# Shifting the activation region of a two-block transformer kernel by 96 bytes, to 512 modulo 1024

## What is computed

```python
# block 1: adaptive norm, three mixers over one input projection, convolutional feed-forward
h = rmsnorm(x, g_attn) * (1 + sc1) + sh1          # the same for the 256 context tokens
cq, ckv, kr, qn, kn, vn, f = split_columns(h @ w_in)
o_mla = blocked_attention(...); o_na = neighborhood_attention(...); o_fn = fourier_mix(f, w_fnet)
x = x + gt1 * (concatenate([o_mla, o_na, o_fn]) @ w_out)
h2 = rmsnorm(x, g_ffn) * (1 + sc2) + sh2
x = x + gt2 * conv_ffn(h2, w_up, conv_w, conv_b, w_down)      # 2048 -> 2*5632 -> 2048
x = rmsnorm(x, g_final)
# block 2: two attention branches, gated merge, SwiGLU
proj = rmsnorm_2(x, norm_mix_g) @ w_in_2
ya = sliding_window_attention(...) @ w_branch_a; yb = stick_breaking_attention(...) @ w_branch_b
x = x + (sigmoid(ga) * ya + sigmoid(gb) * yb) @ w_out_2
x = x + swiglu(rmsnorm_2(x, norm_ffn_g), w_ffn_in, w_ffn_down)
return rmsnorm_2(x, norm_final_g)
```

## Time and profile before

| what | value |
|---|---|
| device time, median of 3 runs (lowest to highest) | 2605.36 us (2604.16 to 2605.7) |
| profiled execution: span from first to last instruction | 2602.8 us |
| TensorE matmul busy | 2578.5 us, 99% |
| weight loads busy (beside the matmuls) | 2212.9 us, 85% |
| VectorE busy | 1763.1 us, 68% |
| ScalarE busy | 1217.6 us, 47% |
| DMA traffic | 548.72 MB, mean 211 GB/s |

### The profile page before, as it was taken

One profiled execution on the slowest core, in us unless ns is written; L12 is line 12 of the kernel. 1 busy time (PEld: TensorE's weight loads), 2 busy tenths in 40 slices (PEclk: granted clock), 3 DMA queues, 4 the chain that ended last, 5 costly groups with the idle time before them and its releaser, 6 DMA issues.

```text
span 2602.8 us, 36329 instructions
## 1 busy us (share of the span) xinstructions
PE 2578.5 (99%) x14852; PEld 2212.9 (85%) x14852; DVE 1763.1 (68%) x2432; ACT 1217.6 (47%) x1602; POOL 33.4 (1%) x30
## 2 busy tenths in 40 slices
PE   8999999999999999999999999999999999999998
PEld 5788778888888888888888888899888888888887
DVE  3377977898888877555656677676766666665444
ACT  4442444455555555444433555545544444444443
POOL 2100000000000000000000000000000000000000
PEclk9999999999999999999999999999999999999999
DMA  9887975677777655555555544465555555555554
GB/s 392 352 308 267 334 249 174 220 247 233 239 238 236 208 191 183 196 190 191 184 190 189 169 140 137 156 194 188 188 190 189 189 190 193 187 188 199 194 194 139
DMA packets 151414, 548.72 MB, mean 211 GB/s; under 512 B 16976, under 2 KB 18896, under 8 KB 150352
## 3 DMA queue, kind: packets, MB, share of 16 engines
q1 hardware_dynamic: 148464, 540.34, 61.4%
q10 hardware_dynamic: 2784, 6.06, 0.8%
HBM read 543.72 MB, written 2.10 MB: 210 GB/s over the span
## 4 chain that ended last, share of the span: by engine, by line
PE 95%; DVE 3%; DMA 1%; ACT 1%; issue 0%; SPq 0%; ACTq 0%; DVEq 0%
PE ps L485 42%; PE ps L484 21%; PE ps L497 5%; PE ps L496 5%; PE ps L495 5%; PE ps L489 3%; PE ps L482 3%; PE ps L491 3%; PE ps L490 3%; PE ps L483 1%; DVE raw L448 1%; PE ps L1783 1%; PE ps L2005 1%; DVE lo L437 1%; PE ps L1974 1%; DMA raw_deep<-in_stream 0%
## 5 line engine op out<-in xcount | busy, mean ns | idle before, releaser
L437 DVE TENSOR_TENSOR lo<-raw,hi 128x1024 fp32r<-128x1024 f32 x815 | 993.1, 1223 | 714.6 <-ACT hi L424 712.5
L485 PE MATMUL ps<-pair,hi 128*128 128x512 f32 x3994 | 1390.8, 392 | 0.0
L424 ACT ACTIVATE hi<-raw 128x1024 fp32r<-128x1024 f32 x815 | 860.4, 1059 | 1056.0 <-PE ps L485 763.9
L484 PE MATMUL ps<-pair,lo 128*128 128x256 f32 x3994 | 1119.4, 280 | 0.0
L485 PEld LDWEIGHTS ps<-pair,hi 128*128 128x128 f32 x3994 | 749.9, 188 | 161.1
L484 PEld LDWEIGHTS ps<-pair,lo 128*128 128x128 f32 x3994 | 750.0, 188 | 6.3 <-issue 2.7
L485 PE MATMUL ps<-hid,hi 128*128 128x512 f32 x688 | 238.7, 392 | 0.0
L484 PE MATMUL ps<-hid,lo 128*128 128x256 f32 x688 | 192.3, 280 | 0.0
L1332 DVE TENSOR_REDUCE tmp<-ps 128x256 f32<-128x512 f32 x244 | 165.5, 683 | 0.4
L485 PEld LDWEIGHTS ps<-hid,hi 128*128 128x128 f32 x688 | 129.1, 188 | 28.4
L448 DVE CUSTOM_DVE_ANT_0 raw<-raw,c_bc 128x1024 f32<-128x1024 f32 x128 | 152.9, 1218 | 0.0
(11 more groups left out here) (360 smaller groups left out, 2575.9 us busy)
## 6 DMA issues: line engine op xcount, KB each, us to landing
raw<-in_stream SPq DMA_DIRECT2D x983, 512.0 KB, 4.1
raw_deep<-in_stream SPq DMA_DIRECT2D x31, 512.0 KB, 10.8
xc<-in_xc SPq DMA_DIRECT2D x4, 1024.0 KB, 8.1
x<-in_x ACTq DMA_DIRECT2D x1, 2048.0 KB, 9.1
c_bc<-in_c_bc SPq DMA_DIRECT2D x1, 1024.0 KB, 10.4
bias<-in_rpb ACTq DMA_DIRECT2D x4, 256.0 KB, 4.5
g_bc<-in_g_bc ACTq DMA_DIRECT2D x1, 1024.0 KB, 4.8
out<-out_sb SPq DMA_DIRECT2D x4, 256.0 KB, 2.7
```

Of the source, the lines that this page charges most:

```text
L424: e.activation(hi[:, c % R, :], raw_of(p), ACT.Copy).then_inc(hi_ready, 1)
L437: e.tensor_tensor(lo[:, c % R, :], raw_of(p), hi[:, c % R, :].bitcast(F32), ALU.subtract)\
L484: e.matmul(out[:, T:2 * T], wlo, act[:, 0, :], start=False, stop=False)
L485: return e.matmul(out, whi, both_, start=False, stop=last)
```

## The change

The area of `pair` moves from 97696 to 97792, and `reg` with it from 130464 to 130560. All tiles that lie over `pair` or at `reg` plus whole kilobytes are now at 512 modulo 1024. The four tiles that were at `reg` plus 96 lose the 96, so that they stay where they were. Nothing else changes: not the rings, `x`, `tmp` or the small tables, and not the order, number or shape of any instruction.

```diff
@@ two_blocks
-        top[0] += (32 - top[0]) % 128
+        top[0] += (512 - top[0]) % K1
 
         pair, both_at = place("pair", [P, KT, 2, T], F32R)
         reg = top[0]
-        assert reg + 96 * K1 + 96 <= nc.sbuf_usable_end, reg + 96 * K1 - nc.sbuf_usable_end
+        assert reg + 96 * K1 <= nc.sbuf_usable_end, reg + 96 * K1 - nc.sbuf_usable_end
...
-        hid2, _ = place("hid2", [P, FT, 2, T], F32R, reg + 96)
-        gate2, _ = place("gate2", [P, 4, T], at=reg + 88 * K1 + 96)
-        val2, _ = place("val2", [P, 4, T], at=reg + 92 * K1 + 96)
-        g_bc, _ = place("g_bc", [P, D], at=reg + 88 * K1 + 96)
+        hid2, _ = place("hid2", [P, FT, 2, T], F32R, reg)
+        gate2, _ = place("gate2", [P, 4, T], at=reg + 88 * K1)
+        val2, _ = place("val2", [P, 4, T], at=reg + 92 * K1)
+        g_bc, _ = place("g_bc", [P, D], at=reg + 88 * K1)
```

## The result

The changed kernel takes 2627.82 us (2625.74 to 2630.08, 4 runs), the kernel before 2604.76 us (2603.95 to 2605.7, 4 runs) beside it. The ratio is 1.0087, 95% interval 1.0076 to 1.0099: 23 us slower, well clear of the noise, where I had forecast 20 us faster. The time lies inside the range of the prediction, at the place of its third rival.

The account below looks back on a forecast made before the run. TensorE's matmul pace was taken as the bound. Gains of 3.7 (`tokens`), 3.9 (`three`) and 12.5 us (`features`), 20.1 in all, took the 2602.8 us span to 2582.7, or 2585 us as median; range 2561 to 2632.

Parts of the forecast that it names:

- Rival 3: In `features`, equal phases of weight load and moving stream collide, 6.5 ns more a couple: 2630 us; chance 0.35.
- The bound: Whole kernel: TensorE is busy 99% of the span, so only the pace of its own matmuls counts.
- `tokens` on the moved tiles: 576 matmuls in `vn`, `f`, `ukv`, `vb` and with `ckvn` get 6.5 ns shorter, 3.7 us less; the surest term.
- `three` with 512 columns: 528 matmuls fall from 234.2 to 226.8 ns, 3.9 us less.
- `three` with 256 columns: No change taken; bounds were 4.4 us less and no change.
- Other engines: ScalarE and VectorE: no address effect worth a term, their edits hidden by the TensorE stream.
- Waits: Tiles are shifted whole, so no new overlap and no new wait.
- the `features` term: 5024 couples of one 256- and one 512-column matmul get 2.5 ns shorter each, 12.5 us less.
- rival 2: All matmuls: once operands are aligned, excess time goes by columns, 45 us less, 2560 us; chance 0.10.
- Rival 1: Matmuls: only the stationary operand's place matters, or neither's; gain 3.7 us or none, 2602 to 2605 us; chance 0.15.

Follow-up runs that it names:

- e5: Changed kernel with all activations, hid2 too, at 544 modulo 1024, 32 bytes modulo 128 from the rings: 2610.86 us.
- e2: Changed kernel with rings and activations all shifted by 32 bytes, so their distance stays 0: 2626.9 us.
- e10: Changed kernel with lo ring and activations at 64 modulo 128, hi ring and hid2 at 0: 2578.15 us.
- e3: Changed kernel with the 512-column matmul ahead of the 256-column one in every couple: 2620.8 us over ten runs (2607.43 to 2623.07).
- e12: Kernel before with the lo ring 32 bytes further and 512 columns ahead of 256 in every couple: 2597.03 us.
- e6: Changed kernel with all activations, hid2 too, at 480 modulo 1024, distance 96 from both rings: 2634.26 us (2626.03 to 2639.91).
- e9: Kernel before with the hi ring shifted by 32 bytes, so distances are 32 for lo and 0 for hi: 2633.0 us.

## Why the prediction was wrong

**What held.** The bound: TensorE is busy in 99%, and 23.7 of the 25.5 us that the span grew are its busy time. The premise that a matmul's cost depends on where its operands lie: e5 and e2 show it, and that it is the distance that counts. Against it I had weighed what the Trainium skill says ("SBUF — State Buffer", "Who interferes with whom"): TensorE has two independent read ports, one for the moving operand and one for weight loads, and never waits on anyone. Taken as a rule on addresses, which it doesn't speak of, it gives 2605 us; measured were 2627.8 and, with another edit of addresses alone, 2578.2. `tokens` on the moved tiles: predicted 3.7 us less, measured 3.8. `three` with 512 columns: predicted 3.9 less, measured 3.2 (14.8 ns of excess on the mean instead of 13.5). `three` with 256 columns was to stay, and became 1.7 us dearer: on `pair` distance 0 makes it 13.2 ns, about as much as for 512 columns. Other engines: no effect, as predicted. Waits: I said none; the profiled execution has 5.1 us more, of which 1.7 are the stretch at 1.2 GHz and 2.5 the longer pause ahead of it. One reading of the rows was less sharp than I took it for: the 355 ns of `kva` are the starts of two couples only, in steps of 10 ns.

**The step that failed** is the `features` term: "the 512 columns fall to the 13.5 of `hid2`, the 256 keep their 10.8, together 24.3, so 2.5 ns a couple, 12.5 us less". Measured is 22.0 and 10.1 on the mean, 5.2 ns a couple more, 25.9 us. So 38 of the 43 us by which I missed lie in this term; the waits (5.1) and `three` (1.7 + 0.7) make the rest, less some 3 us: the two profiled spans lie 25.5 us apart where the medians lie 23.1, and the kernel before took 2604.76 us beside the changed one instead of 2605.36. I carried the price of a matmul in a stream of one width over to a stream of two. That such prices don't add I could have read in the rows of before: by `tokens` and `three` a couple should have cost 233.3 + 117.5 = 350.8 ns, and it cost 346.8. The alternation had a bonus of 4 ns. Rivals 2 and 3 named it, no term of my sum did, and the edit could take it away. I had used the 512-column row of `hid2` and the couple's own 256-column row in one sum, from two different rhythms.

**Rival 3 came true**, nearly to the number: one step of 6.5 ns a couple less what `tokens` and `three` give, 2630 us. It decides from 1.5 ns a couple; it was 5.2 on the mean, since not every group takes the slower pace (about 550 sixes of couples at 353.3 ns, 110 at 346.7). Its nearness to 2630 is in part luck: the step was smaller than its 6.5 ns on the mean, and the waits, which it didn't have, made up for that. The step itself is there, but the reason given for it is only half shown. "Equal phases collide" isn't true as such: streams of one width are at their best with equal phases at 512 columns (226.7 ns), and the best couples of all, in e10, have equal phases on the short matmul. What the runs show is that in alternation the two distances together decide, and not each by itself. Rival 1 (2602 to 2605) and rival 2 (2560) are out.

**What stays open.** Why a given pair of distances has the paces it has (340.0, 344.4, 346.7, 351.7 and 353.3 ns are all held steadily in one run or another), and what at a start chooses where there are two. No run here looks inside the start; e3 and e12 only show that one program can go either way, and the runs of e6 suggest it. Whether the distance acts within a matmul or between a matmul and the load beside it is open, and so is the part of the PSUM banks. The regrouping was tried in one form, and full separation of the widths wasn't tried.

## What to carry to other kernels

A cost per instruction read in a stream of one kind isn't a price that holds in a mixture; before carrying it over, check that such prices add up to the mixture that the trace already shows. Here they missed it by 4 ns of 347, and that was the size of the effect to be forecast. Where TensorE is 99% busy with fp32r matmuls, the byte offset of moving and stationary operands is worth trying as a parameter, each ring by itself: it moved this kernel by +1.1% to -1.0% at no instruction's change, and the best of those tried (256-column ring at distance 0, 512-column ring at 64) wasn't the tidy one. Take several runs of each variant: e3 took 2607 or 2623 us with nothing changed.

## What the runs showed of the hardware

- The cost of an fp32r matmul of 128 x 512 in a stream of its own kind depends on the distance of its operands modulo 128 bytes: 226.7 ns at 0 and 233.3 at 32 in `tokens`, and with 256 columns on `pair` 120.0 and 117.5 in `three`. Shifting both operands by 32 bytes changes nothing (e2, 2626.9 against 2627.8 us).
- Alternating 256- and 512-column matmuls that add up in one bank run at a pace of their own, from 340 to 353 ns a couple by the distances, that isn't the sum of the two streams (350.8 at 32 and 32, where it is 346.7).
- A stream of couples can hold either of two paces with nothing different in its instructions: for whole groups in the changed kernel, and for 770 us without a change in e3.
- In an idle time of TensorE of 3.42 us its granted clock fell to 0.50 for 6.8 us, and matmuls of 512 columns took 427 ns instead of 227 (changed kernel, 297.9 to 304.7 us). With 2.20 us of idle time at the same place it stayed at 1.00 (e2), with 1.86 us it fell (e9), so the length of the idle time alone doesn't decide.
